# First stage of an adaLN hybrid layer: chunk 0's modulation on TensorE, low parts shared with GpSimd, matmuls of ones in waits

## The reference

```python
ada = silu(c) @ w_ada + b_ada                  # 6 x 1024: shift1, scale1, gate1, shift2, scale2, gate2
h = x * (1 + scale1) + shift1                  # x: 256 x 1024, fp32
proj = h @ w_in                                # q k v | hgrn q f i g | gate a, gate b
ya, yb = moba_attention(...), hgrn2(...)
mixed = sigmoid(ga) * (ya @ w_branch_a) + sigmoid(gb) * (yb @ w_branch_b)
x = layer_norm(alpha * x + gate1 * (mixed @ w_out))
h2 = x * (1 + scale2) + shift2
x = layer_norm(alpha * x + gate2 * peer(h2))   # 8 heads, 128 x 128 experts, top 16
```

## Time and profile before

| | us |
|---|---|
| median of 3 runs | 1024.97 (1024.19 to 1026.61) |
| the profiled execution's own time | 1025.29 |
| its span | 1023.5 |
| mean granted clock of TensorE | 0.992 |

### The profile page before, as it was taken

One profiled execution on the slowest core, in us unless ns is written; L12 is line 12 of the kernel. 1 busy time (PEld: TensorE's weight loads), 2 busy tenths in 40 slices (PEclk: granted clock), 3 DMA queues, 4 the chain that ended last, 5 costly groups with the idle time before them and its releaser, 6 DMA issues.

```text
span 1023.5 us, 17998 instructions
## 1 busy us (share of the span) xinstructions
PE 1004.8 (98%) x6863; PEld 929.8 (91%) x6863; DVE 778.7 (76%) x1592; ACT 514.4 (50%) x756; POOL 322.0 (31%) x206
## 2 busy tenths in 40 slices
PE   7999999999999999999999999999999999999996
PEld 7999889989999999999999999988888888888785
DVE  7978888874899698886687788766666867776666
ACT  5785656545444544445444434454554545545443
POOL 2001000011887478777778777000010000000002
PEclk9999999998999999999999999999999999999998
DMA  9879868676555587778766666667779788887761
GB/s 356 354 284 373 288 193 298 250 228 207 169 181 171 160 207 185 186 175 193 168 149 144 149 161 146 180 212 220 217 231 328 225 248 262 265 274 216 222 189 44
DMA packets 96854, 222.80 MB, mean 218 GB/s; under 512 B 27520, under 2 KB 45952, under 8 KB 96000
## 3 DMA queue, kind: packets, MB, share of 16 engines
q1 hardware_dynamic: 74336, 207.93, 62.7%
q0 software_dynamic: 22144, 13.71, 8.9%
q10 hardware_dynamic: 288, 0.01, 0.0%
HBM read 211.06 MB, written 10.55 MB: 217 GB/s over the span
## 4 chain that ended last, share of the span: by engine, by line
PE 93%; DVE 3%; DMA 1%; ACT 1%; POOL 0%; issue 0%; POOLq 0%; ACTq 0%; DVEq 0%
PE px L1161 33%; PE pw L862 17%; PE pw L863 17%; PE pw L864 17%; PE px L1137 3%; DMA ada<-in_ada 1%; PE px L1106 1%; PE pv L862 1%; PE pv L864 1%; PE pv L863 1%; DVE w_lo L1215 0%; DVE part L1264 0%; PE px L862 0%; PE px L863 0%; PE px L864 0%
## 5 line engine op out<-in xcount | busy, mean ns | idle before, releaser
L567 ACT ACTIVATE w_hi<-raw 128x1024 fp32r<-128x1024 f32 x312 | 328.7, 1057 | 317.8 <-PE px L1161 159.9
L1215 DVE TENSOR_TENSOR w_lo<-raw,w_hi 128x1024 fp32r<-128x1024 f32 x285 | 347.3, 1225 | 135.4 <-ACT w_hi L567 133.2
L862 PE MATMUL pw<-a_hi,w_hi 128*128 128x256 f32 x1280 | 368.1, 288 | 0.6 <-DVE a_lo L1482 0.6
L864 PE MATMUL pw<-a_hi,w_lo 128*128 128x256 f32 x1280 | 363.3, 284 | 0.0
L863 PE MATMUL pw<-a_lo,w_hi 128*128 128x256 f32 x1280 | 363.3, 284 | 0.0
L540 POOL DMA_INDIRECT gates_spill<-gate,place x128 | 227.4, 1777 | 83.9 <-issue 46.3
L862 PEld LDWEIGHTS pw<-a_hi,w_hi 128*128 128x128 f32 x1280 | 246.7, 193 | 2.2 <-issue 1.2
L863 PEld LDWEIGHTS pw<-a_lo,w_hi 128*128 128x128 f32 x1280 | 246.9, 193 | 0.1
L864 PEld LDWEIGHTS pw<-a_hi,w_lo 128*128 128x128 f32 x1280 | 246.6, 193 | 0.0
L1161 PE MATMUL px<-w_hi,ws_hi 128*128 128x512 f32 x512 | 158.8, 390 | 0.0
L1161 PE MATMUL px<-w_lo,ws_hi 128*128 128x512 f32 x512 | 158.5, 389 | 0.0
(11 more groups left out here) (348 smaller groups left out, 1154.3 us busy)
## 6 DMA issues: line engine op xcount, KB each, us to landing
raw<-in_u SPq DMA_DIRECT2D x128, 512.0 KB, 4.3
raw<-in_v SPq DMA_DIRECT2D x128, 512.0 KB, 4.8
raw<-in_ws SPq DMA_DIRECT2D x56, 512.0 KB, 5.9
ada<-in_w_ada SPq DMA_DIRECT2D x32, 512.0 KB, 6.9
gates_spill<-zero POOLq DMA_DIRECT2D x16, 512.0 KB, 7.0
g_row<-gates_spill SPq DMA_DIRECT2D x128, 64.0 KB, 4.6
ada<-in_ada SPq DMA_DIRECT2D x6, 1024.0 KB, 10.5
raw<-in_w SPq DMA_DIRECT2D x7, 768.0 KB, 10.6
```

The source lines that it names most:

```text
L567: return nc.scalar.activation(out, in_, ACT.Copy, **kw)
L862: nc.tensor.matmul(out, lh, rh, start=start and x == 0, stop=False)
L864: last = nc.tensor.matmul(out, ll, rh, start=False, stop=stop and x == len(pairs) - 1)
L1215: v.tensor_tensor(w_lo[:, m % RING], raw[:, m % RING], w_hi[:, m % RING].bitcast(F32), ALU.subtract).then_inc(lo_ready, 1)
```

## The change

- Chunk 0's modulation: `sum_part(0)` goes; TensorE multiplies the eight slices of `ada1[0]` with silu(c) as a one-column operand (`mod1_first`, two halves of 8 matmuls). 10 ones matmuls stand before, 2 between, 8 behind it, in place of 20.
- SyncE loads chunk 1's modulation weights ahead of the second half of chunk 0's weights.
- Low parts of the weights: VectorE makes columns 0 to 511 (0 to 767 in chunk 0), GpSimd the rest in two pieces; TensorE waits for them before block 2 and before the last two.
- ScalarE's products (k = 0, 1) go back to VectorE; the early steps are now k below 6. The high part of the second half of chunk 0's weights moves behind h of chunk 0.
- `mod1(c + 1)` stands behind block 1 (in chunk 0 behind block 3).
- The two HI blocks are computed with 128 rows of h as the loaded operand and 512 columns moving (`first_rows`); the copy to `vh` follows the new layout.
- `keep(n, bank)`, n matmuls of ones, in `transposed_x1` (1, 4, 0, 3, 3) and between the halves of the first WQ piece (3).

```diff
@@ -367,8 +367,10 @@
...
                 s = c % CHUNK_SLOTS
-                if c >= CHUNK_SLOTS:
-                    sp.wait_ge(part_ready, c - CHUNK_SLOTS + 1)
+                if c == CHUNK_SLOTS:
+                    sp.wait_ge(mod1_done, 1)
+                if c > CHUNK_SLOTS:
+                    sp.wait_ge(part_ready, c - CHUNK_SLOTS)
@@ -379,6 +381,7 @@
...
                     sp.wait_ge(lo1_ready, c - CHUNK_SLOTS + 1)
+                    sp.wait_ge(lo1_pool_ready, 2 * (c - CHUNK_SLOTS) + 2)
@@ -396,9 +399,11 @@
...
             load_x(0)
+            load_ada1(1)
...
             for c in range(1, KC):
-                load_ada1(c)
+                if c > 1:
+                    load_ada1(c)
@@ -492,6 +497,14 @@
...
+            for c in range(KC):
+                pool.wait_ge(hi1_ready, c + 2)
+                if c >= 2:
+                    pool.wait_ge(chunk_used, c - 1)
+                for q in (slice(FW // 3 if c else FW // 2, 2 * FW // 3), slice(2 * FW // 3, FW)):
+                    nc.gpsimd.tensor_tensor(lo1[c % 2][:, q], raw1[c % CHUNK_SLOTS][:, q], hi1[c % 2][:, q].bitcast(F32),
+                                            ALU.subtract).then_inc(lo1_pool_ready, 1)
@@ -589,27 +602,12 @@
...
                 act.wait_ge(raw1_landed[c % CHUNK_SLOTS], 16 * (c // CHUNK_SLOTS + 1))
-                if c == 0:
-                    q = slice(0, FW // 2)
-                    copy(hi1[0][:, q], raw1[0][:, q]).then_inc(hi1_ready, 1)
-                    act.wait_ge(raw1_head_landed, 16)
-                    q = slice(FW // 2, FW)
-                    copy(hi1[0][:, q], raw1[0][:, q]).then_inc(hi1_ready, 1)
-                    return
...
-            def products(c):
-                s = c % CHUNK_SLOTS
-                act.wait_ge(ada1_landed[s], 16 * (c // CHUNK_SLOTS + 1))
-                act.wait_ge(mod1_done, c - 1)
-                for k in range(2):
-                    last = nc.scalar.activation(part[c % 2][:, k], ada1[s][:, k], ACT.Identity, scale=sc_col[:, k:k + 1])
-                last.then_inc(prod_ready, 1)
-            split_hi1(0)
+            act.wait_ge(raw1_landed[0], 16)
+            copy(hi1[0][:, 0:FW // 2], raw1[0][:, 0:FW // 2]).then_inc(hi1_ready, 1)
@@ -622,10 +620,11 @@
...
                 last.then_inc(h_hi_ready, 1)
+                if c == 0:
+                    act.wait_ge(raw1_head_landed, 16)
+                    copy(hi1[0][:, FW // 2:FW], raw1[0][:, FW // 2:FW]).then_inc(hi1_ready, 1)
...
                     split_hi1(c + 1)
-                if c + 2 < KC:
-                    products(c + 2)
@@ -876,6 +875,8 @@
...
                                            for k in range(half * KC // 2, (half + 1) * KC // 2)], start=half == 0, stop=half == 1)
+                        if half == 0:
+                            keep(3, pw[1])
@@ -911,14 +912,21 @@
...
+            def keep(n, bank):
+                for _ in range(n):
+                    nc.tensor.matmul(bank[:, 0:P], ones_pp[:, :], ones_pp[:, :], start=True, stop=True)
...
                     transposes_x1(0, range(4 * half, 4 * half + 4))
+                    keep((1, 4)[half], pw[1])
...
                     transposes_x1(1, ks)
+                    keep((0, 3, 3)[n], pw[1])
@@ -926,9 +934,17 @@
...
+            def mod1_first(half):
+                for k in range(half * KC // 2, (half + 1) * KC // 2):
+                    for s in range(2):
+                        last = nc.tensor.matmul(px[0][:, s:s + 1], ada1[0][:, k, s * P:(s + 1) * P], sc_col[:, k:k + 1],
+                                                start=k == 0 and s == 0, stop=k == KC - 1 and s == 1)
+                return last
...
-                pe.wait_ge(part_ready, c + 1)
+                pe.wait_ge(part_ready, c)
@@ -939,23 +955,42 @@
...
                     q = slice(s * P, (s + 1) * P)
-                    pair = (a_hi[:, c, q], a_lo[:, c, q], hi, lo) if b in NATURAL else (hi[:, q], lo[:, q], a_hi[:, c], a_lo[:, c])
-                    last = three(p1[b][:, s * T:(s + 1) * T], [pair], start=c == 0 and s == 0, stop=c == KC - 1 and s == 1)
+                    last = three(p1[b][:, s * T:(s + 1) * T], [(hi[:, q], lo[:, q], a_hi[:, c], a_lo[:, c])],
+                                 start=c == 0 and s == 0, stop=c == KC - 1 and s == 1)
...
+            def first_rows(t, c):
+                q, w = slice(t * P, (t + 1) * P), slice(256 * HI, FW)
+                last = three(p1[HI + t][:, :], [(a_hi[:, c, q], a_lo[:, c, q], hi1[c % 2][:, w], lo1[c % 2][:, w])],
+                             start=c == 0, stop=c == KC - 1)
+                if c == KC - 1:
+                    last.then_inc(first_done, 1)
+                return last
             pe.wait_ge(consts, 1)
-            for i in range(20):
-                nc.tensor.matmul(px[3][:, 0:P], ones_pp[:, :], ones_pp[:, :], start=True, stop=True)
-            mod1(0)
+            keep(10, px[3])
+            pe.wait_ge(sc_ready, 1)
+            pe.wait_ge(ada1_landed[0], 16)
+            mod1_first(0)
+            keep(2, px[3])
+            pe.wait_ge(ada1_head_landed, 16)
+            mod1_first(1).then_inc(mod1_done, 1)
+            keep(8, px[3])
...
                 pe.wait_ge(h_lo_ready, c + 1)
-                for b in range(FIRST):
-                    last = first_block(b, c)
-                    if b == 2 and c + 1 < KC:
+                for b in range(HI):
+                    if b == 2:
+                        pe.wait_ge(lo1_pool_ready, 2 * c + 1)
+                    first_block(b, c)
+                    if b == (1 if c else HI - 1) and c + 1 < KC:
                         mod1(c + 1)
+                pe.wait_ge(lo1_pool_ready, 2 * c + 2)
+                for t in range(TT):
+                    last = first_rows(t, c)
@@ -1230,17 +1265,11 @@
...
-                if c == 0:
-                    for h in range(2):
-                        q = slice(h * FW // 2, (h + 1) * FW // 2)
-                        dve.wait_ge(hi1_ready, h + 1)
-                        ins = v.tensor_tensor(lo1[0][:, q], raw1[0][:, q], hi1[0][:, q].bitcast(F32), ALU.subtract)
-                    ins.then_inc(lo1_ready, 1)
-                    return
-                dve.wait_ge(hi1_ready, c + 2)
+                q = slice(0, FW // 3 if c else FW // 2)
+                dve.wait_ge(hi1_ready, c + 2 if c else 1)
...
                     dve.wait_ge(chunk_used, c - 1)
-                v.tensor_tensor(lo1[c % 2][:, :], raw1[c % CHUNK_SLOTS][:, :], hi1[c % 2][:, :].bitcast(F32), ALU.subtract) \
+                v.tensor_tensor(lo1[c % 2][:, q], raw1[c % CHUNK_SLOTS][:, q], hi1[c % 2][:, q].bitcast(F32), ALU.subtract) \
@@ -1248,26 +1277,23 @@
...
                     dve.wait_ge(ada1_landed[s], 16 * (c // CHUNK_SLOTS + 1))
+                    if c >= 2:
+                        dve.wait_ge(mod1_done, c - 1)
                 for k in ks:
-                    if c >= 2 and k < 2:
-                        continue
-                    if c in (0, KC - 1) and k == 4:
-                        dve.wait_ge(ada1_end_landed if c else ada1_head_landed, 16)
+                    if c == KC - 1 and k == 4:
+                        dve.wait_ge(ada1_end_landed, 16)
...
                     else:
-                        if c >= 2 and k < 4:
-                            dve.wait_ge(prod_ready, c - 1)
-                        else:
-                            dve.wait_ge(sum_chain, (6 * c if c < 2 else 12 + 4 * (c - 2) - 2) + k - 1)
+                        dve.wait_ge(sum_chain, 6 * (c - 1) + k - 1)
...
                     if k == KC - 1:
-                        dve.wait_ge(halves_ready, 2 * c + 2)
+                        dve.wait_ge(halves_ready, 2 * c)
@@ -1286,12 +1312,10 @@
...
             v.tensor_scalar(om_lb[:, :], lb_col[:, :], -1.0, 1.0, ALU.mult, ALU.add)
-            early, late = range(4), range(4, KC)
-            sum_part(0, early)
+            early, late = range(6), range(6, KC)
...
                             b_cols[:, :].rearrange("p (k s) -> p k s", s=2)[:, :, 1], 1.0, None, ALU.add).then_inc(b_cols_ready, 1)
-            sum_part(0, late)
```

More of the change, by code:

```diff
@@ L292, in layer @@
             "hi1_ready", "lo1_ready", "part_ready", "mod1_done", "h_hi_ready", "h_lo_ready", "chunk_used", "first_done"))
-        halves_ready = sem("halves_ready")
+        halves_ready, sc_ready, lo1_pool_ready = sem("halves_ready"), sem("sc_ready"), sem("lo1_pool_ready")
         sum_chain, b_cols_ready, mod1_copied = sem("sum_chain"), sem("b_cols_ready"), sem("mod1_copied")
@@ L301, in layer @@
         pool_chain, dve_chain, act_chain = sem("pool_chain"), sem("dve_chain"), sem("act_chain")
-        lb_landed, prod_ready = sem("lb_landed"), sem("prod_ready")
+        lb_landed = sem("lb_landed")
         lb_e_ready, c_sig_ready, lb_max_ready = sem("lb_e_ready"), sem("c_sig_ready"), sem("lb_max_ready")
@@ L645, in _ @@
                 else:
```

(4 more changed lines are left out.)

## The result

The changed kernel takes 1037.25 us (median, 1035.6 to 1042.84) against 1024.9 (1024.19 to 1026.61) on the same chip: ratio 1.0129, 95% interval 1.0109 to 1.015. It is slower by 12 us. The profiled execution took 1036.78 with a span of 1035.0; before it was 1025.29 and 1023.5.

A forecast was written before the change was run, and what follows sets the result against it. VectorE was taken to bound the first stage at 4.97 us a chunk, before DMA's 4.84 and TensorE's 4.74. The terms 12.7 - 1.5 = 11.2 on 1025.3 gave 1036.5 us, own range 1032 to 1042, over all cases 1020.8 to 1041.0.

The forecast's parts named there:

- The lock: First stage: VectorE instructions with two SBUF inputs, sums included, and GpSimd's SBUF reads each wait for the other's whole instruction.
- rival A: First stage: GpSimd works beside VectorE at no cost, DMA bounds at 4.84 us a chunk; 1022.0 us, chance 0.22.
- B: First stage: only low parts, additions and products wait, sums partly slip beside GpSimd, about 5.5 a chunk; 1028.6 us, chance 0.12.
- the `tensor_scalar` of 2.45 us: An earlier trace's VectorE instruction, started at 325.20 and lasting to the end of GpSimd's second subtraction, cited as evidence of waiting.
- 6.9 a chunk: First stage: each chunk costs VectorE's and GpSimd's lists together, 4.45 + 2.45 = 6.9 us against 4.97.
- VectorE's own list: First stage, per chunk: 4.97 - 1.05 for low-part columns given up + 0.53 for products taken back = 4.45 us.
- GpSimd's pair: First stage: GpSimd's two low-part pieces of 512 columns, 2.45 us a chunk with the starts.
- such a drop: First stage: TensorE falls to the lower clock in some chunks, 1.5 to 2 us each; counted only in the range.
- Chunk 0: Start of the first stage: mod1_done near 9.9 instead of 10.7, first matmul near 12.05 instead of 12.95, 0.9 earlier.
- the eight ones: Chunk 0: eight ones matmuls behind the modulation were to fill TensorE's wait before its first matmul.
- Block 6: End of the first stage: block 6 starts at 67.0 against 54.33, 12.7 us later.
- The ones at the layer norm: Before the PEER query: added ones matmuls hold the clock, -1.5 us; if it falls all the same, +1.0.

The follow-up runs named there:

- experiment 2: The changed kernel with the modulation's two running sums in a free PSUM bank, GpSimd's share kept: 1024.67 us, ratio 1.0003 to the kernel before.
- Experiments 4: The kernel before with only GpSimd's share added, two thirds of each low part from chunk 1 on: 1032.85 us, ratio 1.0076.
- experiment 8: The changed kernel with the two products back on ScalarE from chunk 2 on: 1034.25 us, ratio 1.0088 to the kernel before.
- experiments 6: The kernel before with only chunk 0's modulation moved to TensorE, 10 ones matmuls ahead, 2 between, 8 behind: 1025.44 us, ratio 1.0009.
- 11: The kernel before with chunk 0's modulation on TensorE (10 ones ahead, 2 between, 3 behind) and the layer norm stage's ones: 1025.33 us, ratio 1.0009.
- experiment 3: The kernel before with only the layer norm stage's ones matmuls ahead of the PEER query: 1023.96 us, ratio 0.9992.
- 1: The changed kernel with all 1536 columns of the low parts on VectorE again: 1030.41 us, ratio 1.0052 to the kernel before.
- experiment 7: The kernel before with chunk 0's modulation on TensorE and ones spread between the one-column matmuls (9 before, 8 behind): 1026.36 us, ratio 1.0023.

## Why the prediction was right, and where its steps were off

**The lock: right.** The step that decided, sums taken as fully blocked, holds: those that start during a subtraction of GpSimd last up to 1.54 us instead of 0.48. The prediction's rival A (side by side at no cost) falls, as VectorE's steps are held in single rows; B (sums not held) falls with the long sums. The Trainium skill, "SBUF — State Buffer", section "Who interferes with whom", also has the other half, that a VectorE instruction with at most one SBUF input, outside its two-port modes, does not contend with GpSimd; the traces agree: the four sums at 28.59 in experiment 2 take 1.65 us in the middle of GpSimd's pair. The prediction had put the `tensor_scalar` of 2.45 us under that section's sentence on two inputs, but it reads one tensor, as do the products that take 2.70 for 0.60 after. The products wait when they write SBUF (347 ns undisturbed) and not when they write PSUM (478 ns, experiment 2); why the output counts for them is not shown by these runs.

**6.9 a chunk: right only on average.** Five intervals from chunk 1 to 6 sum to 34.7, 6.94 each. But undisturbed ones are 6.45 to 6.6: VectorE's own list is about 4.3 instead of 4.45 (four sums 1.58 from start to start, not 1.70), and GpSimd's pair, forecast to add 2.45, adds the other 2.2. The rest is a low stretch of the clock from 39.8 to 43.2, in which matmuls start 0.21 apart instead of 0.12; it stretches two intervals to 8.06 and 7.14, 2.2 above two undisturbed ones. Experiments 4 and 8 have one such stretch each, too. The prediction had such a drop in its range, not in its sum. So two errors of about 2 us cancelled, and that the average met 6.9 is luck.

**Chunk 0: wrong.** The first matmul was to start at 12.05 and started at 13.97. Two terms failed. The modulation was sized at the full clock. Its second half took 2.42 for 16 records instead of 1.68, as the clock fell at 9.0, and the first took 1.86; mod1_done came at 10.7 instead of 9.9. (The prediction's own terms, 5.6 + 1.68 + 0.4 for two ones + 1.68, add up to 9.4; what the other 0.5 is, it doesn't say.) And the eight ones, which "fill that wait", outlast it: h's low part is done at 12.81, the ones, also at the lower clock, run on for 1.2.

```profile
5.88 1.86 PE px L941 x16
7.74 0.55 PE px L918 x4
8.29 2.42 PE px L941 x16
```

The first fence is the chain of the kernel after; this is its timeline of TensorE:

```profile
10.56 3.76 PE L918 MATMUL px<-ones_pp 128*128 128x128 f32 x16
13.97 0.56 PE L861 MATMUL pw<-a_hi,hi 128*128 128x256 f32 x1
```

By the prediction's own words a first matmul later than 12.95 refutes this part. It cost next to nothing further: in experiments 6 and 11, which start chunk 0 at 13.63 and 12.60, chunk 1 starts at 19.74 and 19.88 (before 19.87). The chain to chunk 1 goes through VectorE.

```profile
12.82 0.53 DVE part L1287 x2
13.34 5.93 DVE part L1290 x6
```

Six sums take 5.93 where they took 2.39: GpSimd's pieces of chunks 0 and 1 lie on them. Chunk 1 started at 22.92, forecast 22.8.

**Block 6: right in the number, by the same luck,** 67.25 against 67.0. The low-clock stretch made up for the shorter list and for chunk 7, which came 5.3 after chunk 6 instead of 5.5.

**The ones at the layer norm: right.** No low clock there. The first transposition of x1 comes 12.92 later than before (239.77), VectorE's copy of iota behind the piece 11.39 later (260.49): -1.53, forecast -1.5. Alone, in experiment 3, the same stretch is 1.54 shorter and the median 0.9 lower. In the kernel after, the second half of the piece begins after h2's low part, not after the ones:

```profile
246.67 0.83 PE L918 MATMUL pw<-ones_pp 128*128 128x128 f32 x6
247.82 0.39 PE L861 MATMUL pw<-a_hi,w_hi 128*128 128x256 f32 x1 [0.32 <-DVE a_lo L1506]
```

**The parts apart.** In medians the share alone makes 1032.85 - 1024.85 = 8.0, chunk 0 1025.44 - 1024.65 = 0.8, the ones -0.9. Experiment 8 would give 3.0 to the products, and the four would make 10.9 of the 12.35 measured, but its trace does not bear the 3.0 out. So of the loss 8.0 is shown to be the share; the rest is not divided. The stretches at the lower clock cost as much as such parts (the one from 39.8 to 43.2 stretches two intervals by 2.2) and differ from kernel to kernel.

**Open.** Why the clock falls during or after the one-column matmuls. The kernel before has a low stretch too, 13.1 to 16.6, after 4.5 us (8.4 to 12.95) in which TensorE had 0.61 of work; six kernels with the one-column stretch (after, 1, 2, 6, 7, 11) have it 3.6 to 5.5 earlier and 6.8 long. The seventh, experiment 8, stays at half pace from the start to 17.4 instead. What experiment 7 excludes is only that ones between the pairs mend it.

## What to carry to other kernels

Before giving GpSimd part of VectorE's work, list VectorE's instructions that read two tensors from SBUF, and the `tensor_scalar` ones from SBUF to SBUF, and count their time and GpSimd's as one queue. Moving an input of the sums and the output of the products to PSUM freed them from the lock, which here was worth 12.6 us, but then check that the gain isn't just the removal of a loss: no kernel with GpSimd's share beats the old one, and the lowest median is the old one's with ones in its waits. Read the longest instruction of a group beside its mean: a wait of a whole instruction falls on few of them. Time saved ahead of an engine that another queue feeds (here the first block) is not time saved.

## What the runs showed that was not expected

- The lock works both ways and in pairs: in experiment 2 GpSimd's pair takes 3.04, half of the earlier trace rows's two is 2.43: its first piece waits for VectorE's 0.69 us low part begun 0.04 before it.
- A `tensor_scalar` of 128 x 256 takes 347 ns from SBUF to SBUF and 478 ns to PSUM; a `scalar_tensor_tensor` 477 and 479.
- TensorE's one-column stretch: 16 records took 1.86 and 2.42 in one execution, the second partly in a stretch at the lower clock, and 3.41 twice in experiment 8 under a granted clock of 1.00; ones between them did not keep it up (8.6 to 15.4 at 0.50).
